# Gate tables in DRAM by blocks of 64 tokens instead of by pieces of 320 tokens

## What is computed

```python
def peer_ffn(h, wq, keys, u_tab, v_tab):          # 8 heads, 128 keys, 16 of them chosen
    ...
    top, pos = lax.top_k(cand, PEER_TOPK)
    eidx = jnp.take_along_axis(cidx, pos, axis=-1)     # 128 experts of 16384 for each token
    g = jax.nn.softmax(top, axis=-1).astype(ht.dtype)
    u = u_tab[eidx]                                    # rows of 1024 floats
    v = v_tab[eidx]
    a = jax.nn.gelu(jnp.einsum('thkd,td->thk', u, ht))
    return jnp.einsum('thk,thkd->td', g * a, v)
```

## Time and profile before

| | us |
|---|---|
| time before, median of 3 runs | 2581.59 |
| lowest and highest of the 3 | 2580.67, 2585.64 |
| the profiled execution: its own time | 2584.99 |
| the profiled execution: its span in the trace | 2583.3 |
| mean granted TensorE clock of the span | 0.951 |

### The profile page before, as it was taken

How to read it: one execution, slowest core, us unless ns; L and a number is a source line. 1 busy time by engine, 2 the same in 40 slices (tenths; PEclk the granted TensorE clock), 3 DMA queues, 4 the chain that set the end, 5 groups by cost and what they waited for, 6 DMA issues and landing times. The chain is left out here.

```text
span 2583.3 us, 32956 instructions
## 1 busy us (share of the span) xinstructions
PE 2335.8 (90%) x13072; PEld 1793.0 (69%) x13072; DVE 1581.7 (61%) x3188; ACT 870.2 (34%) x1617; POOL 863.9 (33%) x653
## 2 busy tenths in 40 slices
PE   8999988997987777779899966899999999999999
PEld 7756655675544444368677855788888888888887
DVE  5358567453101000054536997799889898889986
ACT  3134343432000000033424358644433333333332
POOL 0013221001110001000004448565567766666760
PEclk9999898998999999969998976999999999999999
DMA  5345010246999999842105126899999999999993
GB/s 192 126 173 196 33 66 33 101 175 235 426 426 427 426 426 427 349 166 86 46 33 204 42 82 209 315 413 356 344 403 413 413 413 412 379 404 401 400 400 121
DMA packets 141024, 690.55 MB, mean 267 GB/s; under 512 B 18381, under 2 KB 44789, under 8 KB 107201
## 3 DMA queue, kind: packets, MB, share of 16 engines
q1 hardware_dynamic: 80128, 476.53, 46.3%
q0 software_dynamic: 60736, 211.85, 21.0%
HBM read 657.95 MB, written 37.24 MB: 269 GB/s over the span
## 5 line engine op out<-in xcount | busy, mean ns | idle before, releaser
L3598 PEld LDWEIGHTS psum<-rounded,rounded 128*128 128x128 f32 x2880 | 430.5, 188 | 23.0 <-ACT rounded L3641 11.7
L3598 PE MATMUL psum<-rounded,rounded 128*128 128x320 f32 x2880 | 443.1, 310 | 1.2 <-ACT arena L3163 1.2
L3561 PE MATMUL psum<-rounded,rounded 128*128 128x512 f32 x1536 | 397.6, 395 | 0.0
L3507 POOL DMA_INDIRECT arena<-u_rows,arena x192 | 289.3, 1507 | 161.9 <-DVE arena L3806 50.9
L3507 POOL DMA_INDIRECT arena<-v_rows,arena x192 | 287.7, 1498 | 151.3 <-DVE arena L3817 69.3
L3561 PEld LDWEIGHTS psum<-rounded,rounded 128*128 128x128 f32 x1536 | 283.4, 188 | 76.3 <-issue 14.2
L3683 DVE TENSOR_TENSOR rounded<-arena,rounded 128x1024 fp32r<-128x1024 f32 x247 | 301.2, 1219 | 5.9 <-ACT rounded L3630 5.9
L1707 PE MATMUL psum<-arena 128*64 128x256 f32 x2048 | 234.5, 384 | 59.5 <-DMA arena<-w 58.8
L3630 ACT ACTIVATE rounded<-arena 128x1024 fp32r<-128x1024 f32 x248 | 260.2, 1050 | 10.9 <-DMA arena<-uv 7.7
L1835 DVE COPY arena<-psum 128x256 f32<-128x256 f32 x32 | 13.6, 425 | 407.2 <-PE psum L1774 407.2
L1707 PEld LDWEIGHTS psum<-arena 128*64 128x64 f32 x2048 | 148.7, 138 | 156.4 <-DMA arena<-w 62.5
(11 more groups left out here) (517 smaller groups left out, 3797.5 us busy)
## 6 DMA issues: line engine op xcount, KB each, us to landing
arena<-w SPq DMA_DIRECT2D x96, 2048.0 KB, 42.4
arena<-uv SPq DMA_DIRECT2D x124, 1024.0 KB, 8.5
arena<-wada SPq DMA_DIRECT2D x12, 2048.0 KB, 8.5
arena<-gd SPq DMA_DIRECT2D x30, 640.0 KB, 7.0
gd<-arena SPq DMA_DIRECT2D x18, 1024.0 KB, 9.8
arena<-wp SPq DMA_DIRECT2D x8, 2048.0 KB, 7.9
arena<-win SPq DMA_DIRECT2D x4, 2048.0 KB, 7.6
arena<-wq SPq DMA_DIRECT2D x4, 2048.0 KB, 11.8
```

What stands on the lines that cost most here:

```text
L3507: po.indirect_dma_start(out=ROWS_OF[i % len(ROWS_OF)], out_offset=None, in_=src, in_offset=bass.IndirectOffsetOnAxis(ap=column.bitcast(U32 ...
L3561: ins = pe.matmul(PS[:, 2 * n + half, :], gg[:, z, 128 * n:128 * n + 128], v[:, y, 512 * half:512 * half + 512], x == 0 and i == 0, x == 1 ...
L3598: ins = pe.matmul(PS[:, 7, 0:DT], w[:, y, k, :], hv[:, z, :], k == 0 and i == 0, k == 7 and i == 2)
```

## The change

The scratch tensor is laid out by block of 64 tokens first, then by piece, and the three places that use it follow.

```diff
@@ -2647,7 +2647,7 @@
-    gd = nc.dram_tensor("gd", [128, 32, DT, 4], F32, kind="Internal").ap()
+    gd = nc.dram_tensor("gd", [128, DT // 64, 32, 256], F32, kind="Internal").ap()
@@ -3397,7 +3397,7 @@
     def g_piece(sp, p):
-        sp.dma_start(out=at(GSL[p % 2], 4 * DT), in_=gd[:, p].rearrange("p t r -> p (t r)")).then_inc(*ring[3 + p % 2]("g", p))
+        sp.dma_start(out=at3(GSL[p % 2], DT // 64, 256), in_=gd[:, :, p, :]).then_inc(*ring[3 + p % 2]("g", p))
@@ -3408,7 +3408,7 @@
     def dense_sp(sp):
         def write(x, q):
             a0 = 2 if x > 2 and q == 0 else 8 * q
-            sp.dma_start(out=gd[:, a0:8 * q + 8, 64 * x:64 * x + 64, :], in_=g_of(x)[:, a0:8 * q + 8]).then_inc(*d_gd[x % 2][q]("g", x))
+            sp.dma_start(out=gd[:, x, a0:8 * q + 8, :].rearrange("p a t -> p (a t)"), in_=g_of(x)[:, a0:8 * q + 8].rearrange("p a t r -> p (a t r)")).then_inc(*d_gd[x % 2][q]("g", x))
@@ -3427,7 +3427,7 @@
         for p in range(2):
-            sp.dma_start(out=at3(G_FIRST[p], 192, 4), in_=gd[:, p, 0:192, :]).then_inc(*ring[3 + p]("g", p))
+            sp.dma_start(out=at3(G_FIRST[p], 3, 256), in_=gd[:, 0:3, p, :]).then_inc(*ring[3 + p]("g", p))
```

## The result

The changed kernel takes 2592.68 us (median of 16 runs, all but one between 2587.98 and 2597.62). The kernel before, measured again beside it, takes 2587.89 us (median of 16 runs, 2580.67 to 2593.17); the three runs shown ahead of the prediction were low ones. The one run outside, 2702.18 us, had a granted clock of 0.831 and is left out of the ratio. The ratio is 1.0022, with a 95% interval of 1.0012 to 1.0033: 5.7 us slower, between 3.1 and 8.5. The two medians differ by 4.8 us, which lies in that interval.

The account below looks back on a forecast made before the run. The prediction took TensorE to bound the kernel, with the DMA barely keeping up. Terms of 0 + 0 + 0 + 0 + 3.0 us on the 2581.6 us median gave 2584.6 us, range 2579.5 to 2590.5, counted as no change.

Parts of the forecast that it names:

- step (5): Gate fetch at 1906 us, queued behind xs: gates and then weights land later, TensorE follows, +3.0 us, bounds 0 and 5.6.
- What bounds the kernel: Dense pass: TensorE is the bound, the DMA barely keeps up, and TensorE's cushion is used up only near 1932 us.
- Price of a run: DMA engine time: five 1 KB runs take 0.250 us against 0.202 for one of 5 KB, 0.38 us more per fetch.
- Turns: SP's and GpSimd's queues alternate run by run, so a gate piece with five times the runs gives away 40 turns.
- rival of one turn for a whole fetch: Runs taken many at a time: gates behind xs pass in 3.3 us, +0.4 us, 2582.0 us; chance 0.12.
- Steps (1) and (2): The 20 gate writes, now in longer runs, and the two early gate fetches, landing long before use: 0 us each.
- Step (3): The 29 ordinary gate fetches: land after 12.5 us instead of 6.9, 2.4 us before wanted, so covered: 0 us.
- Step (4): DMA total over the pass: 0.38 us per fetch, 1.3%, rate 408 GB/s against a need of some 409: 0 us.
- The DMA as the bound: From 1930 to 2500 us, 18 fetches cost 6.8 us on top of 3.0, giving 2591.4 us; chance 0.15.
- gates come too late at each fetch: Ordinary gate fetches land beyond 14.9 us after issue; one us beyond at each of 29 gives 2613.6 us; chance 0.05.
- earlier gathers help: Shorter writes start gathers earlier, fewer are queued at 1906 us, up to 1 us gained, 2580.6 us; chance 0.02.

Follow-up runs that it names:

- a_xs42: Changed kernel with the 2 MB fetch of xs sent ahead of raw piece 42 instead of 40; ratio to the kernel before 0.9998 (0.9982 to 1.0015).
- a_split: Changed kernel with xs fetched in eight DMAs of 256 KB, one behind each of raw pieces 42 to 49; ratio 0.9999 (0.9986 to 1.0013).
- a_run5k: Changed kernel with its 29 later gate fetches taken as one 5 KB run per partition again (wrong gates), writes kept at 8 KB; ratio 1.0001 (0.9990 to 1.0012).
- b_run1k: Kernel before with its 30 later gate fetches taken as five 1 KB runs per partition (wrong gates), writes still 1 KB; ratio 1.0034 (1.0020 to 1.0047).
- b_split: Kernel before with xs fetched in eight DMAs of 256 KB, one behind each of raw pieces 42 to 49; ratio 0.9994 (0.9982 to 1.0005).
- a_runs10: Changed kernel with later gate fetches as ten 512 B runs per partition (wrong gates); traced once, pass 954.0 us, 20.5 more than before.

## Why the prediction was wrong

The forecast of 2584.6 us and its range up to 2590.5 missed the 2592.68 us. The direction of its single term and its place were right; its size was not (step (5) below, 3.0 us where the trace has 5.7), and the time it was added to was 6.3 us too low. Of the 8.1 us between the forecast and the measured median, 6.3 are this base and 1.8 the term, by the difference of the medians.

- **What bounds the kernel: right.** TensorE is the bound, one event has no cushion, and the loss is in that event alone (balance of the pass; `a_xs42`, `a_split`).
- **Price of a run: right for writes, a little high for fetches.** Writes got cheaper, as reckoned. With the writes in runs of 8 KB, the window of the earlier trace rows at 1560 us moves 210 GB/s at a share of 0.51, or 0.0389 ns for a byte and engine, against 0.0488:

```profile
1560.00:1580.00 20.00, 10.76 (x125) 9.10 (x122) 19.38 (x45) 19.22 (x45) 13.18 (x9) 0.75 0.51 210
```

  For a fetch the packets in the traces give the price: at the event the 640 packets of 1 KB took 47 ns each on average, the 128 of 5 KB in the kernel before 200 ns. Five short ones cost 237 ns, so a fetch costs 8 x 0.037 = 0.3 us more, where the prediction took 0.38. None of it reached TensorE by itself.
- **Turns: right.** The waits follow the number of runs (1, 2, 5, 10), and writes of other sizes change nothing. The rival of one turn for a whole fetch falls: it allowed 0.4 us of idle time more, and 4.2 were measured. The packets tell one run at a time from eight or nine as well: 99% of the gathered runs are followed at once by one of SP's. At the ceiling that the Trainium skill gives (DMA: Bandwidth & Descriptors, Queues, rings and completion order) 0.4 us would have been lost; this trace does not agree with that end.
- **Steps (1) and (2), the writes at 0 us: right** (`a_run5k`, 1.0001). That GpSimd waits a few us less for them is not shown: with writes in 1 KB runs it waited 17.1 us (before) and 24.6 us (`b_run1k`, `b_split`), with 8 KB runs between 15.9 us (`a_split`) and 22.3 us (`a_run5k`).
- **Step (3), ordinary fetches at 0 us: right**, and so is its working. VectorE waits for gates at none of them. In the eight fetches between 1972 and 2186 us the last packet ended 11.5 to 12.6 us after the issue, where it was 6.3 to 7.1 before; the landing comes 0.6 to 0.7 us behind that in the kernel before. The prediction had 12.5 us to landing. `a_runs10` shows the other side, where four of them are late.
- **Step (4), the DMA's total at 0 us: right**, with little to spare (one wait of 0.44 us for rows in `a_xs42`).
- **Step (5), +3.0 us: the step that failed.** It was mis-sized twice. First, the idle time grew by 4.16 us, not 3.0. The prediction let the gathers run out after four row sets, so that the weights would pass in 2.6 us; from the use of the gates to the use of the weights it was 1931.20 - 1927.86 = 3.3 us. Its own count was 10.7 us at 2.2 us for a set, or 4.9 sets, and it took four. It also took the gather at 1920.28 for the last; the trace of the kernel before has one more, and the changed kernel issues it at the same place, 23.52 us after xs. These are the lines of before, then of after:

```profile
1922.57 0.94 POOL L3507 DMA_INDIRECT arena<-u_rows,arena  x1 [0.30 <-issue]
```
```profile
1920.97 0.94 POOL L3507 DMA_INDIRECT arena<-u_rows,arena  x1 [0.30 <-issue]
1930.24 1.43 POOL L3507 DMA_INDIRECT arena<-u_rows,arena  x1 [8.34 <-DVE arena L3811]
```

  The packets count what was still queued. From the last packet of xs to that of the gates (1919.75 to 1927.06 us), and from there to that of the weights (1927.1 to 1930.5 us), GpSimd's queue moved this much in the changed kernel:

```profile
q0 software_dynamic: 550, 2.00, 70.0%
```
```profile
q0 software_dynamic: 118, 0.42, 31.1%
```

  That is 2.42 MB, or 4.6 row sets of 0.52 MB, and the 0.42 MB beside the weights stand where the prediction had none. The second miss was left out altogether: what a stall of this length does to the clock, 1.58 us. Idle time was priced as time lost and no more. The trace of the kernel before had this price too: at the start of the pass TensorE idles for 3.51 us, the granted clock behind it is 0.50, and the eight matmuls of L3531 take 1.94 us instead of 1.04, the six of L3561 behind them 2.22 instead of 1.55, together 1.57 us:

```profile
1645.50 2.22 PE L3561 MATMUL psum<-rounded,rounded 128*128 128x512 f32 x6
...
1643.90:1646.70 2.80, 2.80 (x11) 2.61 (x12) 1.03 (x1) 0.82 (x1) 0.00 (x0) 0.50 0.96 349
```

  With both, step (5) is 5.7 us in the profiled execution, the ratio's own value, of which the interval runs from 3.1 to 8.5.
- **The base.** The forecast stood on 2581.59 us, the median of three runs. Sixteen runs give 2587.89. The profiled execution, at 2585.0, was nearer, and the prediction noted the gap of 3.4 us and chose the median. By the kernel's own base the forecast would have been 2590.9, and 2592.68 would lie inside a range moved by the same 6.3 us. The loss of 5.7 us lies at the prediction's upper bound of 5.6, which held idle time alone.
- **Rivals.** The DMA as the bound gave 2591.4, close to the measured time, and is nevertheless wrong: `a_xs42` keeps every short run and loses nothing. That gates come too late at each fetch, and that earlier gathers help, did not happen.

## What to carry to other kernels

A transfer's price is not only its bytes: where two queues feed the same DMA engines run by run, cutting one fetch into more runs lets the other queue pass ahead, and everything behind the fetch in its own queue is later by that much. Look for the one place where the cushion is already used up (here 2 MB of unhurried traffic ahead of urgent weights) and price the change there; then spread or move that traffic, which here made the cut free. And when a stall of several us is forecast for TensorE, add the slow matmuls after it, and take the base from as many runs as there are.

## What the runs showed of the hardware

The granted clock fell to half with idle times of 2.60, 4.52, 4.98, 5.81 and 5.96 us in the dense pass, and not with 0.36, 0.83, 1.38, 1.40 and 1.55 us, though TensorE had run at full speed for 150 us or more before each of the first five. It also fell with the 3.5 us at the start of the pass, in all ten traces. In the changed kernel it fell at TensorE's restart; in `b_run1k` it was already at half 2.1 us before the restart at 1945.74. These are the half-speed windows of `b_run1k`, and of `a_runs10` after its idle time of 2.60 us:

```profile
1943.60:1950.40 6.80, 4.66 (x18) 3.00 (x19) 6.80 (x12) 3.48 (x6) 4.26 (x3) 0.50 0.84 312
```
```profile
2111.70:2115.00 3.30, 3.30 (x15) 3.30 (x14) 3.30 (x6) 1.56 (x3) 2.04 (x2) 0.50 1.03 416
```

The other surprise is how large a single idle event is beside 29 longer fetches: ScalarE waited for weights in 15 places instead of two, and only the one behind xs was paid.
